# Low-operand terms swept last, an opening in smaller transfers, and 32-column products ahead of two slabs

## The reference

```python
def first_block(x, ...):
    x = x + 0.5 * swiglu(rms_norm(x, ffn1_norm), w_gate, w_up, w_down)      # f1u, f1d
    z = rms_norm(x, mix_norm) @ w_in + b_in                                 # wq ... wg
    y_attn = sliding_window_attention(...) @ w_proj_attn                    # pa
    y_mlstm = gated_normed_mlstm(...) @ w_proj_mlstm                        # pm
    x = x + (g0 * y_attn + g1 * y_mlstm) @ w_out                            # wo
    return rms_norm(x + 0.5 * swiglu(rms_norm(x, ffn2_norm), ...), final)   # f2u, f2d

def second_block(x, mem, ...):
    proj = rms_norm_2(x, norm_mix) @ w_in                                   # w2, ukv, uq, gg
    h = x + concat(gla(...), latent_attention(...)) @ w_out                 # wo2
    h = h + cross_attention(rms_norm_2(h, norm_xa), mem) @ xa_w_o           # xk, xq, xv, xo
    g = conv3(rms_norm_2(h, norm_ffn) @ w_gate)                             # f3u, f3d
    return h + (silu(g) * (rms_norm_2(h, norm_ffn) @ w_up)) @ w_down
```

## Time and profile before

| what | value |
|---|---|
| median of 3 runs | 970.25 us (969.28 to 970.3) |
| the profiled execution's own time | 969.66 us |
| its span | 967.9 us, granted TensorE clock 1.00 |
| TensorE matmuls busy | 958.4 us, 99%, 8270 matmuls |
| VectorE (DVE) | 690.9 us, 71% |
| ScalarE (ACT) | 535.1 us, 55% |
| GpSimd (POOL) | 130.6 us, 13% |
| HBM traffic | 170.39 MB read, 177 GB/s over the span |

### The profile page before, as it was taken

How to read it: one execution, slowest core, us unless ns; L and a number is a source line. 1 busy time by engine, 2 the same in 40 slices (tenths; PEclk the granted TensorE clock), 3 DMA queues, 4 the chain that set the end, 5 groups by cost and what they waited for, 6 DMA issues and landing times.

```text
span 967.9 us, 20459 instructions
## 1 busy us (share of the span) xinstructions
PE 958.4 (99%) x8270; PEld 941.9 (97%) x8270; DVE 690.9 (71%) x1081; ACT 535.1 (55%) x775; POOL 130.6 (13%) x85
## 2 busy tenths in 40 slices
PE   7999999999999999999999999999999999999998
PEld 7999999999999999999999999989999999999998
DVE  4766766477869968877767655687697688788752
ACT  6545455345658964465545465587575665455441
POOL 0111110010026100002111102400002022223100
PEclk9999999999999999999999999999999999999999
DMA  7776575555454454575666665245245355665761
GB/s 246 220 211 205 183 239 180 181 156 186 151 197 153 136 170 134 177 257 178 206 189 208 207 226 161 90 146 169 88 144 169 125 175 168 191 205 173 251 205 66
DMA packets 169086, 172.37 MB, mean 178 GB/s; under 512 B 5684, under 2 KB 166974, under 8 KB 168894
## 3 DMA queue, kind: packets, MB, share of 16 engines
q1 hardware_dynamic: 169006, 171.45, 55.4%
q10 hardware_dynamic: 16, 0.00, 0.0%
HBM read 170.39 MB, written 1.06 MB: 177 GB/s over the span
## 4 chain that ended last, share of the span: by engine, by line
PE 95%; DVE 3%; DMA 1%; ACT 1%; issue 0%; POOL 0%; SPq 0%; DVEq 0%
PE acc L727 84%; PE part L773 1%; PE acc L773 1%; PE part L813 1%; DMA xraw<-in_x 1%; PE part L837 1%; PE part L1120 1%; PE part L823 1%; DVE wl L474 1%; DVE al L1902 0%; PE part L857 0%; PE part L1110 0%; PE part L1316 0%; PE part L1297 0%; PE part L1143 0%; PE part L936 0%
## 5 line engine op out<-in xcount | busy, mean ns | idle before, releaser
L455 ACT ACTIVATE wh<-raw 128x1024 fp32r<-128x1024 f32 (+2 forms) x292 | 316.9, 1111 | 269.8 <-PE acc L727 111.2
L474 DVE TENSOR_TENSOR wl<-raw,wh 128x1024 fp32r<-128x1024 f32 (+3 forms) x294 | 391.6, 1372 | 55.3 <-ACT wh L455 52.8
L727 PE MATMUL acc<-ah,wh 128*128 128x256 f32 x1520 | 424.4, 279 | 0.4
L727 PE MATMUL acc<-al,wh 128*128 128x256 f32 x1520 | 420.5, 277 | 0.0
L727 PE MATMUL acc<-ah,wl 128*128 128x256 f32 x1520 | 420.4, 277 | 0.0
L727 PEld LDWEIGHTS acc<-ah,wh 128*128 128x128 f32 x1520 | 285.3, 188 | 4.4 <-issue 3.1
L727 PEld LDWEIGHTS acc<-al,wh 128*128 128x128 f32 x1520 | 285.2, 188 | 0.1
L727 PEld LDWEIGHTS acc<-ah,wl 128*128 128x128 f32 x1520 | 285.2, 188 | 0.0
L2770 POOL TENSOR_TENSOR sil<-sil,rstd 128x512 f32<-128x512 f32 x33 | 62.0, 1879 | 306.7 <-ACT sil L1423 215.2
L727 PE MATMUL acc<-hh,wh 128*128 128x256 f32 x352 | 97.4, 277 | 0.0
L727 PE MATMUL acc<-hl,wh 128*128 128x256 f32 x352 | 97.2, 276 | 0.0
(11 more groups left out here) (445 smaller groups left out, 1528.0 us busy)
## 6 DMA issues: line engine op xcount, KB each, us to landing
raw<-in_ffn_w_up SPq DMA_DIRECT2D x33, 1024.0 KB, 5.4
raw<-in_ffn_w_down SPq DMA_DIRECT2D x24, 1408.0 KB, 6.2
raw<-in_w_in SPq DMA_DIRECT2D x33, 1024.0 KB, 5.3
raw<-in_ffn_w_gate SPq DMA_DIRECT2D x32, 1024.0 KB, 5.4
raw<-in_w_out SPq DMA_DIRECT2D x8, 1024.0 KB, 5.0
raw<-in_w_proj_attn SPq DMA_DIRECT2D x4, 1024.0 KB, 4.9
raw<-in_w_proj_mlstm SPq DMA_DIRECT2D x4, 1024.0 KB, 5.0
raw<-in_xa_w_kv SPq DMA_DIRECT2D x4, 1024.0 KB, 4.9
```

Of the source, the lines that this page charges most:

```text
L455: nc.scalar.activation(wh[:, slot, a * nw:b * nw], raw[:, slot, a * nw:b * nw], ACT.Copy).then_inc(S("w_hi"), 1)
L474: nc.vector.tensor_tensor(wl[:, slot, a * nw:b * nw], raw[:, slot, a * nw:b * nw], f(wh[:, slot, a * nw:b * nw]), SUB).then_inc(S("w_lo"), 1)
L727: ins = mm(dst, a, b, start=st and q == 0, stop=en_ and q == 2, skip_group_check=True)
```

## The change

- The opening. Constants: 128 columns instead of 256. x still comes in quarters on SP's queue, with the last quarter of the first slab before the last of x; the other three quarters of that slab are issued by ACT's queue. The second slab (`u[:, :, 0:256]`) comes in two halves. TensorE runs 3 turning products on a tile of ones that DVE sets, before the constants are there, 3 behind the transposed gains, and 1 behind each of the first two quarters, none later. `first_slab` lets TensorE do chunks 0 and 1 of the slab before it transposes the last quarter of x. ACT and DVE split the first slab in quarters.
- `product` gets `high`: with it the matmuls of a half slab are swept as q = 0, 2 for all its chunks, waiting for the operand's high halves, and then q = 1, waiting for its low halves. It is used in n5's first slab, in both parts of xo's first product, and in n8's first slab.
- `own`: a 32-column product into the slab's own accumulator, overwritten by the slab's first matmul; ahead of the attention projection's slabs 0 and 2.
- ACT and DVE split half 0 of w2's second slab before the last norm part of n5 instead of behind it, and the high half of an 8-chunk slab's first half waits only for the first half of an 11-chunk slab.
- POOL's second addition of squares in n8 waits for all four low halves.

The diff's changed lines (context left out):

```diff
@@ -451,7 +451,9 @@
-                    slab_used(act, s - 2, i, half if shape_of(s - 2) == (nk, nw) and s - 2 not in EXTRA else 1)
+                    same = shape_of(s - 2) == (nk, nw) and s - 2 not in EXTRA
+                    shorter = shape_of(s - 2) == (11, 256) and (nk, nw) == (8, 256) and half == 0
+                    slab_used(act, s - 2, i, half if same or shorter else 1)
@@ -479,15 +481,14 @@
-            sp.dma_start(cst[:, 0:256], consts[:, 0:256]).then_inc(S("ident"), 16)
+            sp.dma_start(cst[:, 0:P], consts[:, 0:P]).then_inc(S("ident"), 16)
-            for half in range(2):
-                for j in (2 * half, 2 * half + 1):
-                    c = slice(j * 256, (j + 1) * 256)
-                    sp.dma_start(xraw[:, :, c], xrows[:, :, c]).then_inc(S(f"x_in{j}"), 16)
-                sp.dma_start(raw[:, 0, half * 1024:(half + 1) * 1024].rearrange("p (k c) -> p k c", k=4),
-                             gate1[:, 4 * half:4 * half + 4, 0:256]).then_inc(S("raw0" if half else "raw_first"), 16)
+            for j in range(4):
+                c = slice(j * 256, (j + 1) * 256)
+                if j == 3:
+                    sp.dma_start(raw[:, 0, 1536:2048].rearrange("p (k c) -> p k c", k=2), gate1[:, 6:8, 0:256]).then_inc(S("raw0"), 16)
+                sp.dma_start(xraw[:, :, c], xrows[:, :, c]).then_inc(S(f"x_in{j}"), 16)
@@ -565,9 +566,11 @@
-                    load(1, 0, u[:, :, 0:256])
+                    for half in range(2):
+                        sp.dma_start(raw[:, 1, half * 1024:(half + 1) * 1024].rearrange("p (k c) -> p k c", k=4),
+                                     u[:, 4 * half:4 * half + 4, 0:256]).then_inc(S("raw1" if half else "raw_second"), 16)
-                    sp.dma_start(cst[:, 256:C_ALL], consts[:, 256:C_ALL]).then_inc(S("consts"), 16)
+                    sp.dma_start(cst[:, P:C_ALL], consts[:, P:C_ALL]).then_inc(S("consts"), 16)
@@ -642,6 +645,28 @@
+            def quarter_in(j):
+                pe.wait_ge(*signal(f"x_in{j}", 16))
+                transpose_in(xraw, "x_ps", X_BANKS, (j,))
+            def first_slab(k):
+                if k == 0:
+                    pe.wait_ge(*signal("first_lo", 1))
+                if k == 2:
+                    quarter_in(3)
+                    lo_ready(pe, 0, 0, 0)
+                if k == 4:
+                    pe.wait_ge(*signal("fourth_lo", 1))
+                if k == 6:
+                    lo_ready(pe, 0, 0, 1)
+                normed_input("n1")(k)
+            def high_input(st):
+                return lambda k: k % 2 == 0 and pe.wait_ge(*signal(st + "_hi", k // 2 + 1))
@@ -695,25 +720,31 @@
-                        before=None, width=P, part=None, used=(1, 1), nw=256, c0=0, narrow=None):
+                        before=None, width=P, part=None, used=(1, 1), nw=256, c0=0, narrow=None, high=None, own=False):
-                    lo_ready(pe, s, i, half)
-                    for k in range(ka, kb):
-                        if before is not None:
+                    if before is not first_slab:
+                        lo_ready(pe, s, i, half)
+                    sweeps = ((0, 1, 2),) if high is None else ((0, 2), (1,))
+                    for sweep, k in [(sweep, k) for sweep in sweeps for k in range(ka, kb)]:
+                        if sweep == (0, 2):
+                            high(k)
+                        elif before is not None:
+                        if own and k == 0:
+                            mm(o[0:32, 0:T], wh[:, slot, c0:c0 + 32], xh[:, k0, :], start=True, stop=True, skip_group_check=True)
-                            st = first and k == 0 and m == 0
-                            en_ = last and k == nk - 1 and m == 1
+                            st = first and k == 0 and m == 0 and sweep[0] == 0
+                            en_ = last and k == nk - 1 and m == 1 and sweep == sweeps[-1]
@@ -723,8 +754,9 @@
-                            for q, (a, b) in enumerate(three):
-                                ins = mm(dst, a, b, start=st and q == 0, stop=en_ and q == 2, skip_group_check=True)
+                            for q in sweep:
+                                a, b = three[q]
+                                ins = mm(dst, a, b, start=st and q == 0, stop=en_ and q == sweep[-1], skip_group_check=True)
@@ -733,7 +765,8 @@
-                product(s, 0, 8, n, xh, xl, before=normed_input(st))
+                product(s, 0, 8, n, xh, xl, before=first_slab if st == "n1" else normed_input(st),
+                        high=high_input(st) if st == "n8" else None)
@@ -839,14 +872,16 @@
+            def turning(n):
+                for _ in range(n):
+                    mm(Q[0][:, 0:P], stmp[:, 0, 0:P], stmp[:, 0, 0:P], start=True, stop=True, skip_group_check=True)
+            pe.wait_ge(*signal("warm", 1))
+            turning(3)
-            def turning(n):
-                for _ in range(n):
-                    mm(Q[0][:, 0:P], ident, ident, start=True, stop=True, skip_group_check=True)
@@ -857,12 +892,11 @@
-            turning(2)
-            for j in range(4):
-                pe.wait_ge(*signal(f"x_in{j}", 16))
-                transpose_in(xraw, "x_ps", X_BANKS, (j,))
-                if j % 2:
-                    turning(3)
+            turning(3)
+            for j in range(3):
+                quarter_in(j)
+                if j < 2:
+                    turning(1)
@@ -991,7 +1025,7 @@
-                product(SLAB0["pa"] + k, 0, 8, ACC0["pa"] + k, eh, el, before=normed_input("at") if k == 0 else None)
+                product(SLAB0["pa"] + k, 0, 8, ACC0["pa"] + k, eh, el, before=normed_input("at") if k == 0 else None, own=k in (0, 2))
@@ -1058,7 +1092,7 @@
-            product(s, 0, 8, n, ah, al, before=normed_input("n5"), width=64)
+            product(s, 0, 8, n, ah, al, before=normed_input("n5"), high=high_input("n5"), width=64)
@@ -1334,7 +1368,8 @@
-                    product(s, 0, 4, n + k, mh, ml, before=normed_input("xo") if k == 0 else None, part=part,
+                    product(s, 0, 4, n + k, mh, ml, before=normed_input("xo") if k == 0 else None,
+                            high=high_input("xo") if k == 0 else None, part=part,
@@ -1439,6 +1474,8 @@
+                if st == "n3":
+                    split_hi(act, s + 9, only=0)
@@ -1462,16 +1499,25 @@
-            def split_hi_first(half):
-                if half:
-                    loaded(act, 0)
-                nc.scalar.activation(wh[:, 0, half * 1024:(half + 1) * 1024], raw[:, 0, half * 1024:(half + 1) * 1024],
-                                     ACT.Copy).then_inc(S("w_hi"), 1)
+            gate1 = A["ffn1_w_gate"][0].rearrange("(k p) c -> p k c", p=P)
+            def first_load(ka, kb, sem):
+                act.dma_start(raw[:, 0, ka * 256:kb * 256].rearrange("p (k c) -> p k c", k=kb - ka),
+                              gate1[:, ka:kb, 0:256]).then_inc(S(sem), 16)
+            def first_split(ka, kb, sem):
+                A_(wh[:, 0, ka * 256:kb * 256], raw[:, 0, ka * 256:kb * 256], ACT.Copy).then_inc(S(sem), 1)
-            act.wait_ge(*signal("ident", 16))
-            A_(root[:, 2:4], ones[:, 0:2], ACT.Sqrt).then_inc(S("roots"), 1)
+            first_load(0, 2, "raw_first")
+            first_load(2, 4, "raw_third")
+            first_load(4, 6, "raw_fourth")
+            act.wait_ge(*signal("warm", 1))
+            A_(root[:, 2:4], stmp[:, 0, 0:2], ACT.Sqrt).then_inc(S("roots"), 1)
+            act.wait_ge(*signal("raw_first", 16))
+            first_split(0, 2, "first_hi")
@@ -1482,13 +1528,18 @@
+            act.wait_ge(*signal("raw_third", 16))
+            first_split(2, 4, "w_hi")
-            act.wait_ge(*signal("raw_first", 16))
-            split_hi_first(0)
-            split_hi_first(1)
+            act.wait_ge(*signal("raw_fourth", 16))
+            first_split(4, 6, "fourth_hi")
+            loaded(act, 0)
+            first_split(6, 8, "w_hi")
-            split_hi(act, 1)
+            act.wait_ge(*signal("raw_second", 16))
+            A_(wh[:, 1, 0:1024], raw[:, 1, 0:1024], ACT.Copy).then_inc(S("w_hi"), 1)
+            split_hi(act, 1, only=1)
@@ -1626,7 +1677,7 @@
-            split_hi(act, s + 1)
+            split_hi(act, s + 1, only=1)
@@ -1998,6 +2049,8 @@
+                    if st == "n3" and q == 3:
+                        split_lo(dve, s + 9, only=0)
@@ -2075,6 +2128,7 @@
+            V.memset(stmp[:, 0, 0:P], 1.0).then_inc(S("warm"), 1)
@@ -2088,11 +2142,19 @@
+            def first_rest(ka, kb, made, sem, count=1):
+                c = slice(ka * 256, kb * 256)
+                dve.wait_ge(*signal(made, count))
+                V.tensor_tensor(wl[:, 0, c], raw[:, 0, c], f(wh[:, 0, c]), SUB).then_inc(S(sem), 1)
+            first_rest(0, 2, "first_hi", "first_lo")
+            first_rest(2, 4, "w_hi", "w_lo")
-            split_lo(dve, 0, only=0)
-            split_lo(dve, 0, only=1)
+            first_rest(4, 6, "fourth_hi", "fourth_lo")
```

(5 more changed lines are left out.)

## The result

| | before | after |
|---|---|---|
| median of 9 runs | 970.25 us (969.03 to 975.92) | 965.55 us (965.07 to 966.75) |
| ratio, 95% interval | | 0.9939 (0.9915 to 0.9963) |
| profiled execution, its span | 969.66, 967.9 | 965.9, 964.2 |

Between the two profiled executions the difference is 3.7 us, against a forecast sum of 2.35. The direction was right, the size too small, and most of what was missing lies in the opening.

What follows compares the result with a forecast made beforehand. TensorE, busy 99%, bounds the kernel. Gains 1.1 + 0.45 + 0.6 + 0.2 = 2.35 us give 967.3 from the profiled execution or 967.9 by the median; predicted 967.6 us, range 965.0 to 970.3.

Steps and rivals of the forecast that it cites:

- Turning on ones: Opening: three products ahead of the constants, in TensorE's idle time, worth nothing by themselves.
- the 1.1 that I had for the transfers: Opening: x's third quarter lands earlier, so the first slab ends at 17.1; gain 1.1 us, bounds -0.4 and 2.8.
- Rival (b): Opening: TensorE's high level is reached with the first products; the opening gives 2.4, time 966.3 us; chance 0.18.
- The low level lasts until 12.4.: Opening: TensorE keeps half pace until 12.4 as before, so 2.6 us do 11.5 of 48 matmuls.
- the 0.227 of my sum: Opening: assumed time in us of one matmul at half pace, used for the products before 12.4.
- The third quarter: Opening: x's third quarter lands at 8.9, bounds 7.9 and 10.0; first matmul 0.9 us earlier than before.
- rival (d): Opening: two queues alternate, filling no gap; x's third quarter lands at 10.0, gain 0.45, time 968.2 us; chance 0.11.
- n5: Stage after the second feed-forward: the stall before its second slab goes; gain 0.45 us, bounds 0.2 and 0.55.
- Cross-attention's output: Output product (xo): sweeping low halves last removes two stalls; gain 0.6 us, bounds 0.3 and 0.7.
- n8: Last feed-forward: 0.76 of stalls go, about 0.6 returns waiting for the sum; gain 0.2 us, bounds -0.3 and 0.8.
- The alternation of DVE and POOL: Last feed-forward: POOL's additions and DVE's weight low halves take turns, so POOL's last add ends at 790.9.
- 32-column products: Ahead of two slabs: 96 matmuls speed up, 0.43 us, but the next stage waits anyway; 0, bounds -0.1 and 0.1.

Runs made afterwards that it cites:

- the fourth execution of the old opening: Changed kernel with the opening of the kernel before; the first slab's second half starts at 13.34 us; no timed result given.
- the one-queue run: Changed kernel with the first slab's three quarters moved from ACT's queue to SP's; its second half starts at 13.82 us; no timed result given.

## Why the prediction was right and wrong

- **Turning on ones, priced at nothing: the step that failed.** "Nothing by itself" came from asking only what waits for these products. What they do is bring TensorE's full pace forward. Without them after's opening has its second half at 14.20: against the 15.2 of before's three executions that is 1.0, the 1.1 that I had for the transfers (0.5, if the fourth execution of the old opening is counted). The rest, 1.9 to the mean of 12.3, is the share of the ones in this opening. Rival (b) had this course at 0.18, with nearly the right size (2.4).
- **"The low level lasts until 12.4."** It was read from one execution as if it were a time. The level came by 6.4, by 8.4, and at 7.7, 9.5 and 12.8 in five openings. A matmul at the low level costs 0.213, not the 0.227 of my sum, which changes little.
- **The third quarter**, 8.16 in after (bounds 7.9 to 10.0, taken 8.9). Taken from 9.51 the step of 0.6 was right by luck. In seven executions of the old opening the quarter landed between 8.30 and 9.47, mean 8.8, so my starting point was its latest; with two queues it landed between 7.83 and 8.71, mean 8.2. On one queue it landed at 8.45, inside both ranges, so neither the second queue nor the smaller pieces are shown as the cause. The 10.0 of rival (d) fell.
- **n5**: 0.47 against 0.45, from the earlier split, as worked out.
- **Cross-attention's output**: 0.72 by the two stalls against 0.6. A further 0.3 came from the pace, with no edit of the change behind it. And I closed the term there, and did not ask where TensorE would arrive too early next. That was n8, whose first slab, with its own code unchanged, took 0.26 back.
- **n8**: forecast 0.2 for sweep and hold; measured against the run with neither, -0.19, near my lower bound of -0.3. The alternation of DVE and POOL was foreseen, and rightly: the last addition ended 8.6 behind n8's start, forecast 8.7, and the wait for the sum was 0.3, not 0.6. Two terms failed. The first slab took 5.95, not 5.65. And the sum ended at the wait for the sum: DVE's list, 0.4 late behind it, stalls TensorE at the fifth slab for 0.27 to 0.48, which stood in no term.
- **32-column products**: 0, as forecast. TensorE arrives early and waits for DVE, as I had it, but the first such wait is already ahead of slab 2.
- **Not in the forecast at all**: the slow course of the kernel before. My sum was made against a profiled execution in its favourable course, and the median of nine runs holds three of the other, which is 0.6 of the 4.7. A flip of the pace was on my list of ways to be wrong, but only as a risk of the change.

## What to carry to other kernels

Price early throwaway work on TensorE by what it does to the pace of the work behind it, and take an opening's times from several executions before a term of 2 us is built on them. When an edit lets an engine arrive earlier, follow it to the next place where it meets another engine: half of a gain can be given back there. And before a difference of 0.2 us between two executions is put down to an edit, look whether the pace of the same matmuls differs: here it was the pace, twice.

## What the runs showed of the hardware

- The granted clock fell to 0.50 in the middle of real products, behind gaps of 0.61 and 1.15 us (matmuls of 0.21 from 9.2 to 12.6 in the one-queue run), while gaps of 0.33 and 1.11 at the same places left it at 1.00 in another. At the start of a program the column shows 1.00 while transposes take 216 ns, twice the 109 of later ones.
- TensorE has a second, much smaller step, 113.3 against 117.8 ns, at an unchanged clock. In three traces the slow one began with a start 2 to 9 ns late and lasted for 160 us (36 half slabs and all of the down projection) without a single idle moment in the trace. In three others, after's two among them, a slow stretch ended at a stall of 0.27 or 0.28 us.
- POOL's additions and DVE's weight halves slow each other: an addition of 128x512 took 1.76 instead of 1.29 us and four halves 6.89 instead of 5.16.
- The same kernel's first real product starts between 11.74 and 12.41 us (before) and 8.68 and 8.97 (after), as x's quarters land: under the old opening the third quarter's transposes began between 8.35 and 9.51.
